# Second block's first mixer: another order of its projections, and the values' projection dealt out between attention steps

## The chip, the cores and the metric

The kernel runs on one core of one Trainium2 chip. The metric is the device time of one execution in microseconds (us), the median of the timed runs. A core has TensorE (PE: matrix products into the eight banks of PSUM), VectorE (DVE), ScalarE (ACT), GpSimd (POOL) and SyncE (SP), each with its own instruction stream, and 16 DMA engines that move data between DRAM and the on-chip SBUF. The streams meet at semaphores only.

## The reference, cut to what matters

Two blocks of a transformer follow each other; the first has two layers (l = 0, 1) and 256 tokens beside 256 context tokens, width 1024. A layer is: feed-forward, mixer, feed-forward. The change is in the mixer of layer l = 1 ("M1"):

```
qx, kx, vx, ux = split(hx @ w_in, 4)          # 512 columns each; g = 0, 1, 2, 3 below
kc, vc = split(hc @ w_in[:, 512:1536], 2)     # the context: keys and values only, in layer 1
qx, kx = axial_rope(qx), axial_rope(kx)
out = concat([attention(qx, kx, vx, kc, vc, rpb), pool_mix(ux)]) @ w_out
```

The attention has 8 heads of 64, 256 queries against 256 + 256 keys, with a bias table and a mask. `pool_mix` takes windowed means of u and multiplies each of four groups by a 128x128 matrix.

## The kernel before, in words

**Weights.** All weights come in one stream of units of 1 MB (a matrix of 512 columns is two units, the upper and the lower 512 rows). SP loads a unit into one of two `raw` buffers (`fetch`, L2807), ScalarE makes its high part (L1255) and VectorE its low part (L1883). High and low parts have three buffers (CUT = 3). A load into a `raw` buffer waits for the low part made from what was there; a cut waits until the unit three places ahead is used up. Each engine's program calls `through()` where a unit is used up, and makes there the cuts that this permits. So a cut stands in order between the engine's other work, and the place of the `through()` call sets when it comes.

**Products.** Each projection tile is 128 tokens by 512 columns: 8 parts (k steps) of three matmuls (L542 to L544: low x high, high x low, high x high). Tiles 0 and 1 are tokens, 2 and 3 context. In M1 the values and keys have four tiles, the queries and the pool input two.

**Order in M1.** `MIX_ORDER = (2, 0, 1, 3)`: values first (their tiles lie between the transposes of the boundary before, `begin`), then queries, then keys (`project`), and the pool input (g = 3) is dealt out in parts between attention steps (`u_part`). `U_AT[1] = [6, 3, 4, 3]` says how many of the 16 parts come ahead of what TensorE does in step -1, 0, 1, 2. Queries and keys of tokens are rotated: VectorE multiplies by cosines and sines (`rot`, L2200 and L2207, in the buffers XN), POOL adds the two (L2739), TensorE transposes (L832, called by `flush`), ScalarE copies to QT and KT (L1471).

**Attention.** 16 items (head, 128 queries) in 8 steps of two. In step j TensorE makes the scores of items 2j and 2j + 1 (L852), the transposes of the probabilities of items 2j - 4 and 2j - 3 (L861), and in every second step a block of products with the values (L876). VectorE adds the bias and takes the maximum (L2234 to L2242), ScalarE exponentiates (L1501), and the division is VectorE's for even heads (L2251) and ScalarE's for odd ones (L1511). The attention output is cut by ScalarE (L1543) and VectorE (L2258) over the projection's input, so it waits for the last part of the pool input. The pool's four groups stand at steps `POOL_AT[1]` = 5 and the following ones. ScalarE makes the weight cuts that a step's parts permit behind that step, VectorE behind the next one (`late`).

**POOL in M1** (its `mixer`, L2731): sums for g = 0 once rotated, then the store of a gate vector to DRAM (`gate_store`, L2709: 1024 elements of 4 bytes), then twelve loads of bias blocks (L2753, 128 KB each), the load of the pool's matrices (L2756), then the sums for g = 1. VectorE masks the bias blocks (L2215) when all have landed.

**Product behind it.** The output product of M1 follows; its four weight units are cut during the attention.

Of the kernel before, what the change touches and what calls it, by code (L numbers as in the profile page):

```python
# [167 lines left out]

MIX_ORDER = (2, 0, 1, 3)
U_AT = [[6, 2, 4, 4] + [2] * 8, [6, 3, 4, 3]]  # L170


POOL_AT = [12, 5]
EARLY = 11
# [28 lines left out]
def weight_stream(a):  # L203
# [62 lines left out]
    for l in range(2):  # L266
        push_gu(gu1[l, 0], (l, 0))
        push_down(dn1[l, 0], (l, 0))
        for g in MIX_ORDER:
# [28 lines left out]
def build(nc, a, out):  # L298
    with ExitStack() as ctx:
# [232 lines left out]
        def tensor_program(e):  # L532
# [289 lines left out]
            def mixer(l):  # L822
                n_items = 32 if l == 0 else 16
                tts = [[0, 1, 2, 3] if l == 0 or g in (1, 2) else [0, 1] for g in range(4)]
                later = []
# [10 lines left out]

                assert len(tts[MIX_ORDER[0]]) == 4
                first_unit[0] = feed.count
                begin(f"M{l}", lambda t: project_tile(f"M{l}", ("pj", l, MIX_ORDER[0]), t, t == 3))
                for g in MIX_ORDER[1:3]:  # L840
# [6 lines left out]
                def scores(n):  # L847
                    h, qt = items[n]
                    p0, hp, k0 = 64 * (h % 2), h // 2, 0 if qt < 2 else 256
                    b = bank(("sc", l, n))  # L850
                    w.wait_ge(*A.at(("tt", l, 1, tts[1][-1])))
# [55 lines left out]

                start, got, banks, last = feed.count, {}, {}, tts[3][-1]

                def u_part(p):  # L910
                    t, kt = p // 8, p % 8
                    if kt == 0:
                        banks[t] = bank(("pj", l, 3, t))
                    if kt // 4 not in got:
                        got[kt // 4] = unit(4, 512, kt // 4 - (feed.count - start))
                    n, (hi, lo) = got[kt // 4]
                    i = mm3(banks[t], (Hhi[:, kt, 128 * t:128 * t + 128], Hlo[:, kt, 128 * t:128 * t + 128]),
                            (hi[:, kt % 4, :], lo[:, kt % 4, :]), kt == 0, kt == 7)
                    if kt == 7:
                        ring.full(("pj", l, 3, t))  # L920
                        i.then_inc(*T.up(("pj", l, 3, t), *[("unit", n)] if t == last else []))
# [324 lines left out]
        def scalar_program(e):  # L1246
# [215 lines left out]
            def mixer(l):  # L1462
                n_items = 32 if l == 0 else 16
                tts = [[0, 1, 2, 3] if l == 0 or g in (1, 2) else [0, 1] for g in range(4)]
                later = []
# [9 lines left out]
                def evac(g, t):  # L1475
                    f = ("pj", l, g, t)
                    if g < 2 and t >= 2:
                        w.wait_ge(*T.at(f))
                        if g:
                            w.wait_ge(*T.at(("tt", l, 0, t))) if l == 0 else None  # L1480
# [7 lines left out]
                for g in MIX_ORDER[:3]:  # L1488
                    project(lambda t: evac(g, t), tts[g], flush, g != MIX_ORDER[0])
                    if g < 2:  # L1490
                        later.extend((g, t) for t in tts[g])
# [73 lines left out]
                def u_part(p):  # L1565
                    t, kt = p // 8, p % 8
                    if t == tts[3][-1] and kt % 4 == 3:
                        through()
# [23 lines left out]
                for i in range(-1, len(steps) + 3):  # L1592
                    done = range(p, p + (U_AT[l][i + 1] if i + 1 < len(U_AT[l]) else 0))
                    p = done.stop
                    if i < 0:
                        flush()
                    else:
                        for q in done:
                            if q % 8 == 7:
                                evac(3, q // 8)  # L1600
                        step(i)

                        for q in done:
                            u_part(q)

# [265 lines left out]
        def vector_program(e):  # L1871
# [306 lines left out]
            def project(evac, tts, ticks):  # L2178
                for u in range(2):
                    for t in tts:  # L2180
                        if ticks:
                            mod_steps(feed.tick())
                        if u:
                            evac(t)
                    through()

            def mixer(l):
                n_items = 32 if l == 0 else 16
                tts = [[0, 1, 2, 3] if l == 0 or g in (1, 2) else [0, 1] for g in range(4)]

                def evac(g, t):
# [3 lines left out]
                    w.wait_ge(*T.at(f))  # L2195
                    if g:
                        w.wait_ge(*G.at(("z", l, 0, t)))
                    w.wait_ge(*LD["rest"].at("rest"))
# [18 lines left out]

                for g in MIX_ORDER[:3]:
                    project(lambda t: evac(g, t), tts[g], g != MIX_ORDER[0])
                    if g == 1:  # L2220
                        masked(0)
# [47 lines left out]
                def u_part(p):  # L2269
                    if p // 8 == tts[3][-1] and p % 4 == 3:  # L2270
                        through()
# [414 lines left out]
        def gpsimd_program(e):  # L2686
# [44 lines left out]
            def mixer(l):  # L2731
                tts = [[0, 1, 2, 3] if l == 0 or g in (1, 2) else [0, 1] for g in range(4)]

                def evac(g):
                    for t in range(2):
                        w.wait_ge(*V.at(("rot", l, g, t)))
                        if g:
                            w.wait_ge(*T.at(("tt", l, 0, t)))
                        e.tensor_tensor(ZQ[t], XN[t][:, 0:512], XN[t][:, 512:1024], ALU.add).then_inc(  # L2739
# [4 lines left out]
                w.wait_ge(*LD["rpb"].at("rpb"))  # L2744
                evac(0)
                if l:
# [10 lines left out]
                if l == 0:  # L2757
# [217 lines left out]
```

## Time and profile before

| | us |
|---|---|
| median of 3 timed runs (2496.41 to 2496.72) | 2496.54 |
| profiled execution | 2497.18 |
| its span | 2495.4 |
| TensorE busy, share of the span | 2412.9, 97% |
| VectorE, ScalarE, GpSimd busy | 65%, 41%, 14% |
| mean granted clock of TensorE | 0.992 |

The time of an execution lies 1.8 us above its span. A timeline row gives start, duration, engine, line, operation, output<-inputs, shape and count, and in brackets the idle time before it with what released it. Matmuls are pipelined: a row of 0.39 us may be followed by the next after 0.23 us. M1 lies between 1360 and 1478 us of the span. The granted clock is a share of 2.4 GHz.

### The profile page before, as it was taken

What the parts mean: (1) busy time and instruction counts of PE and PEld (TensorE: products, weight loads), DVE (VectorE), ACT (ScalarE), POOL (GpSimd) and SP (SyncE); (2) the same over time, 40 slices, a digit from 0 to 9 for tenths busy, and PEclk for the clock granted to TensorE, in tenths of its full rate; (3) what the DMA queues carried; (4) which work ended last, traced back from release to release, by engine and by line L of the source; (5) the groups of instructions that cost most, each with busy time, mean ns of one, the idle gap of its engine ahead of it and who ended that gap; (6) DMA issues with size and microseconds to landing.
All of it is one profiled execution on the core that took longest, in us unless ns stands there. A gap on an engine that the chain in (4) does not pass through costs nothing.

```text
span 2495.4 us, 29343 instructions
## 1 busy us (share of the span) xinstructions
PE 2412.9 (97%) x12118; PEld 2004.8 (80%) x12118; DVE 1613.3 (65%) x2208; ACT 1021.2 (41%) x1431; POOL 338.9 (14%) x226
## 2 busy tenths in 40 slices
PE   7999989999999999999999989999999999999998
PEld 5887878857888778888888758887888888887987
DVE  7778686374778787543385466756566576586674
ACT  4221325365312225322225464445555544465443
POOL 0334252200143252101030200000000000000000
PEclk9999999999999999999999999999999999999999
DMA  8555552511555553544362615555544355443554
GB/s 284 185 171 184 171 173 96 156 34 57 164 174 181 164 174 120 165 138 152 103 219 92 148 52 193 186 186 163 184 128 159 118 193 190 153 142 119 187 186 142
DMA packets 242629, 385.93 MB, mean 155 GB/s; under 512 B 10880, under 2 KB 150400, under 8 KB 242432
## 3 DMA queue, kind: packets, MB, share of 16 engines
q1 hardware_dynamic: 236320, 372.43, 45.5%
q0 software_dynamic: 6176, 11.64, 2.4%
q8 instruction: 95, 1.56, 0.3%
q14 instruction: 38, 0.31, 0.0%
HBM read 382.83 MB, written 3.11 MB: 155 GB/s over the span
## 4 chain that ended last, share of the span: by engine, by line
PE 67%; DVE 17%; DMA 9%; ACT 4%; issue 3%; POOL 0%; DVEq 0%; SPq 0%; ACTq 0%
PE ps L542 17%; PE ps L544 16%; PE ps L543 16%; PE ps L548 8%; DVE arena L1906 8%; DMA raw<-in_w_mod 6%; PE ps L549 4%; DVE wlo L1883 3%; ACT whi L1255 2%; DVE arena L1903 1%; PE ps L617 1%; PE ps L876 1%; DMA grow<-gcol 1%; DMA raw<-in_w_ffn_gate_up 1%; PE ps L852 0%
## 5 line engine op out<-in xcount | busy, mean ns | idle before, releaser
L1255 ACT ACTIVATE whi<-raw 128x2048 fp32r<-128x2048 f32 x279 | 532.9, 1910 | 1122.3 <-PE ps L544 492.7
L1883 DVE TENSOR_TENSOR wlo<-raw,whi 128x2048 fp32r<-128x2048 f32 x279 | 663.3, 2378 | 489.3 <-ACT whi L1255 489.0
L542 PE MATMUL ps<-wlo,Hcut 128*128 128x512 f32 (+1 forms) x1888 | 706.2, 374 | 21.4 <-DVE Hcut L2087 13.1
L544 PE MATMUL ps<-whi,Hcut 128*128 128x512 f32 (+1 forms) x1888 | 695.9, 369 | 0.0
L543 PE MATMUL ps<-whi,Hcut 128*128 128x512 f32 (+1 forms) x1888 | 695.4, 368 | 0.0
L542 PEld LDWEIGHTS ps<-wlo,Hcut 128*128 128x128 f32 x1888 | 357.1, 189 | 89.3 <-DVE Hcut L2087 15.4
L544 PEld LDWEIGHTS ps<-whi,Hcut 128*128 128x128 f32 x1888 | 356.9, 189 | 59.8
L543 PEld LDWEIGHTS ps<-whi,Hcut 128*128 128x128 f32 x1888 | 357.4, 189 | 56.3
L542 PE MATMUL ps<-Hcut,whi 128*128 128x512 f32 (+1 forms) x1032 | 395.2, 383 | 4.9 <-DVE wlo L1883 4.9
L544 PE MATMUL ps<-Hcut,whi 128*128 128x512 f32 (+1 forms) x1032 | 394.6, 382 | 0.0
L543 PE MATMUL ps<-Hcut,wlo 128*128 128x512 f32 (+1 forms) x1032 | 394.4, 382 | 0.0
L548 PE MATMUL ps<-Hcut,whi 128*128 128x512 f32 x864 | 305.8, 399 | 0.0
L1906 DVE SCALAR_TENSOR_TENSOR arena<-raw,sc,arena 128x512 f32<-128x512 f32 x392 | 276.4, 765 | 35.1 <-DMA raw<-in_w_mod 33.1
L2696 POOL PARTITION_ALL_REDUCE arena<-arena x56 | 205.0, 3703 | 568.6 <-DVE arena L1906 376.0
L549 PE MATMUL ps<-Hcut,wlo 128*128 128x256 f32 x864 | 242.7, 281 | 0.0
L542 PEld LDWEIGHTS ps<-Hcut,whi 128*128 128x128 f32 x1032 | 193.7, 188 | 43.1 <-issue 4.2
L544 PEld LDWEIGHTS ps<-Hcut,whi 128*128 128x128 f32 x1032 | 193.5, 188 | 38.1
L543 PEld LDWEIGHTS ps<-Hcut,wlo 128*128 128x128 f32 x1032 | 193.7, 188 | 37.7
L548 PEld LDWEIGHTS ps<-Hcut,whi 128*128 128x128 f32 x864 | 162.4, 188 | 40.2
L549 PEld LDWEIGHTS ps<-Hcut,wlo 128*128 128x128 f32 x864 | 163.2, 189 | 0.0
L2110 DVE TENSOR_REDUCE arena<-ps 128x256 f32<-128x512 f32 x108 | 73.7, 687 | 23.5 <-PE ps L549 23.4
L2156 DVE TENSOR_TENSOR arena<-arena,ps 128x512 f32<-128x512 f32 x60 | 39.7, 682 | 71.9 <-PE ps L544 71.5
(269 smaller groups left out, 1806.9 us busy)
## 6 DMA issues: line engine op xcount, KB each, us to landing
raw<-in_w_ffn_gate_up SPq DMA_DIRECT2D x88, 1024.0 KB, 5.1
raw<-in_w_mod SPq DMA_DIRECT2D x65, 1024.0 KB, 5.2
raw<-in_w_ffn_down SPq DMA_DIRECT2D x44, 1024.0 KB, 4.9
raw<-in_ffn_w_in SPq DMA_DIRECT2D x44, 1024.0 KB, 5.1
raw<-in_attn_w_in SPq DMA_DIRECT2D x36, 1024.0 KB, 5.1
raw<-in_ffn_w_out SPq DMA_DIRECT2D x22, 1024.0 KB, 4.9
raw<-in_w_in SPq DMA_DIRECT2D x16, 1024.0 KB, 5.1
raw<-in_mlstm_w_in SPq DMA_DIRECT2D x12, 1024.0 KB, 5.1
```

The source lines that it names most:

```text
L542: e.matmul(o, L[0], R[1], start=start, stop=False)
L543: e.matmul(o, L[1], R[0], start=False, stop=False)
L544: return e.matmul(o, L[0], R[0], start=False, stop=stop)
L548: e.matmul(b, L[0], Hcut[:, 0, k, :], start=start, stop=False)
L549: return e.matmul(b[:, 256:512], L[1], SHORT[0][:, k, :], start=False, stop=stop)
L617: i = e.transpose(b[:, 128 * k:128 * k + 128], XS[t][:, o:o + 128], ident())
L1255: e.activation(hi_of(n), slot(n), ACT.Copy).then_inc(*A.up(("hi", n)))
L1883: e.tensor_tensor(lo_of(n), slot(n), hi_of(n).bitcast(F32), ALU.subtract).then_inc(*V.up(("lo", n)))
L1906: i = e.scalar_tensor_tensor(out=o, in0=kslot(n)[:, k, :], scalar=c, in1=o, op0=ALU.mult, op1=ALU.add)
L2110: return e.tensor_reduce(o, bk(f).rearrange("p (s n) -> p n s", s=2), AX, ALU.add)
L2156: e.tensor_tensor(AV[:, 2 * j + s, :], XN[s][:, 0:N], bk(f)[:, 0:N], ALU.mult).then_inc(*V.up(("mul", P, 2 * j + s), ("free", f)))
L2696: e.partition_all_reduce(t, t, 128, bass.bass_isa.ReduceOp.add).then_inc(*G.up(("total", l, v, h, s)))
```

## The change

In M1 the order becomes keys, queries, values, pool input. Only the first two are projected whole (`WHOLE[1] = 2`); the 32 parts of the values and the 16 of the pool input are dealt out as 8, 8, 8, 8, 4, 6, 6 parts ahead of TensorE's steps -1 to 5. The pool's groups move one step later. The buffers for the rotated sums are now written first by the keys and then by the queries, so the waits between them change places (`early_g`, `late_g`), on POOL too: the keys' sums, the gate's store, the bias blocks, the pool's matrices, the queries' sums. VectorE's rotations of the first projection now stand ahead of the first `through()`. The first block's mixer keeps its order, parts and steps.

```
-MIX_ORDER = (2, 0, 1, 3)
-U_AT = [[6, 2, 4, 4] + [2] * 8, [6, 3, 4, 3]]
-POOL_AT = [12, 5]
+MIX_ORDER = [(2, 0, 1, 3), (1, 0, 2, 3)]
+WHOLE = [3, 2]
+U_AT = [[6, 2, 4, 4] + [2] * 8, [8, 8, 8, 8, 4, 6, 6]]
+POOL_AT = [12, 6]
...
+        def part_tiles(l):
+            tts = [[0, 1, 2, 3] if l == 0 or g in (1, 2) else [0, 1] for g in range(4)]
+            return tts, [(g, t) for g in MIX_ORDER[l][WHOLE[l]:] for t in tts[g]]
...
+                order = MIX_ORDER[l]
+                early_g, late_g = [g for g in order if g < 2]
...
                 def u_part(p):
-                    t, kt = p // 8, p % 8
+                    (g, t), kt = tiles[p // 8], p % 8
+                    last, u = tts[g][-1], 2 * (g - tiles[0][0]) + kt // 4
                     if kt == 0:
-                        banks[t] = bank(("pj", l, 3, t))
-                    if kt // 4 not in got:
-                        got[kt // 4] = unit(4, 512, kt // 4 - (feed.count - start))
+                        banks[t] = bank(("pj", l, g, t))
+                    if u not in got:
+                        got[u] = unit(4, 512, u - (feed.count - start))
...
-                    else:
-                        for q in done:
-                            if q % 8 == 7:
-                                evac(3, q // 8)
+                    for q in done:
+                        if q % 8 == 7:
+                            evac(*tiles[q // 8])
+                    if i >= 0:
                         step(i)
...
-                        if u:
+                        if u if ticks else u == 0:
                             evac(t)
...
-                evac(0)
+                evac(early_g)
                 if l:
                     gate_store(1, 8)
...
-                evac(1)
+                evac(late_g)
```

## Rows read from the trace of the kernel before

**Rows 1.** Waits of TensorE, 1380 to 1500: total, times, longest

```profile
PE ps L861 <- ACT arena L1511: 7.9, 4, 3.2
```

**Rows 2.** Timeline of TensorE, 1395 to 1475

```profile
1405.28 1.03 PE L832 MATMUL ps<-cst,arena 128*128 128x128 f32 x8
...
1409.57 0.39 PE L542 MATMUL ps<-wlo,Hcut 128*128 128x512 f32 x1
...
1410.25 0.39 PE L542 MATMUL ps<-wlo,Hcut 128*128 128x512 f32 x1
...
1425.03 1.13 PE L852 MATMUL ps<-arena 64*128 64x512 f32 x4
...
1446.42 3.54 PE L876 MATMUL ps<-arena 128*64 128x256 f32 x16
...
1466.24 1.95 PE L876 MATMUL ps<-arena 128*64 128x256 f32 x16
...
1472.75 0.50 PE L542 MATMUL ps<-wlo,Hcut 128*128 128x512 f32 x1
```

**Rows 3.** Timeline of VectorE, 1370 to 1475

```profile
1377.20 2.29 DVE L1883 TENSOR_TENSOR wlo<-raw,whi 128x2048 fp32r<-128x2048 f32 x1 [1.03 <-ACT whi L1255]
...
1394.74 0.68 DVE L2200 TENSOR_TENSOR arena<-ps,cst 128x512 f32<-128x512 f32 x1
...
1396.00 0.68 DVE L2200 TENSOR_TENSOR arena<-ps,cst 128x512 f32<-128x512 f32 x1
...
1397.26 2.42 DVE L1883 TENSOR_TENSOR wlo<-raw,whi 128x2048 fp32r<-128x2048 f32 x1
...
1427.38 0.96 DVE L2215 TENSOR_TENSOR arena<-arena,cst 128x768 f32<-128x768 f32 x1 [5.83 <-DMA arena<-rpbs]
1428.44 0.42 DVE L2234 TENSOR_TENSOR arena<-ps,arena 128x256 f32<-128x256 f32 x1
...
1429.84 0.41 DVE L2234 TENSOR_TENSOR arena<-ps,arena 128x256 f32<-128x256 f32 x1
```

**Rows 4.** Timeline of ScalarE, a weight cut

```profile
1381.33 1.92 ACT L1255 ACTIVATE whi<-raw 128x2048 fp32r<-128x2048 f32 x1 [2.46 <-PE ps L544]
```

**Rows 5.** Timeline of POOL, 1114 to 1115 and 1340 to 1475

```profile
1114.25 0.90 POOL L2713 DMA_DIRECT2D grow<-gcol  x1 [14.58 <-DVE gcol L1954]
...
1396.25 4.59 POOL L2739 TENSOR_TENSOR arena<-arena 128x512 f32<-128x512 f32 x2 [29.05 <-DVE arena L2207]
1400.78 0.98 POOL L2713 DMA_DIRECT2D grow<-gcol  x1
1401.75 8.17 POOL L2753 DMA_DIRECT2D arena<-rpbs  x12
```

**Rows 6.** Line 2816, four single loads: start, then us to landing (not for 1385.6)

```profile
L2816 SPq DMA_DIRECT2D raw<-in_w_ffn_gate_up x1: 368/368/368, 1113.7 to 1113.7; - x1
...
DMA to landing us min/median/max: 5.7/5.7/5.7
...
L2816 SPq DMA_DIRECT2D raw<-in_w_mod x1: 368/368/368, 1121.8 to 1121.8; - x1
...
DMA to landing us min/median/max: 9.7/9.7/9.7
...
L2816 SPq DMA_DIRECT2D raw<-in_w_in x1: 367/367/367, 1385.6 to 1385.6; - x1
...
L2816 SPq DMA_DIRECT2D raw<-in_w_out x1: 368/368/368, 1409.8 to 1409.8; - x1
...
DMA to landing us min/median/max: 17.4/17.4/17.4
```

**Rows 7.** Two windows: busy by engine, granted clock, DMA share, GB/s

```profile
1406.00:1408.00 2.00, 2.00 (x12) 1.67 (x11) 0.52 (x1) 2.00 (x3) 2.00 (x4) 1.00 0.57 10
1447.00:1450.00 3.00, 3.00 (x16) 1.33 (x13) 2.93 (x9) 0.75 (x2) 0.00 (x0) 0.50 0.34 103
```

**Rows 8.** DMA issues of the page: count, KB each, median us to landing

```profile
raw<-in_w_in SPq DMA_DIRECT2D x16, 1024.0 KB, 5.1
```

More of the change, by code:

```diff
@@ L268, in weight_stream @@
         push_down(dn1[l, 0], (l, 0))
-        for g in MIX_ORDER:
+        for g in MIX_ORDER[l]:
             push(("cols", a["w_in"][l], 512 * g), "cut")
@@ L823, in mixer @@
                 n_items = 32 if l == 0 else 16
-                tts = [[0, 1, 2, 3] if l == 0 or g in (1, 2) else [0, 1] for g in range(4)]
+                tts, tiles = part_tiles(l)
+                order = MIX_ORDER[l]
+                early_g, late_g = [g for g in order if g < 2]
                 later = []
@@ L835, in flush @@
                     later.clear()
-                assert len(tts[MIX_ORDER[0]]) == 4
+                assert len(tts[order[0]]) == 4
                 first_unit[0] = feed.count
-                begin(f"M{l}", lambda t: project_tile(f"M{l}", ("pj", l, MIX_ORDER[0]), t, t == 3))
-                for g in MIX_ORDER[1:3]:
+                begin(f"M{l}", lambda t: project_tile(f"M{l}", ("pj", l, order[0]), t, t == 3))
+                if order[0] < 2:
+                    later.extend((order[0], t) for t in tts[order[0]])
+                for g in order[1:WHOLE[l]]:
                     project(("pj", l, g), tts[g], flush)
@@ L919, in u_part @@
                     if kt == 7:
-                        ring.full(("pj", l, 3, t))
-                        i.then_inc(*T.up(("pj", l, 3, t), *[("unit", n)] if t == last else []))
+                        ring.full(("pj", l, g, t))
+                        i.then_inc(*T.up(("pj", l, g, t), *[("unit", n)] if t == last else []))
                     elif kt == 3 and t == last:
@@ L1463, in mixer @@
                 n_items = 32 if l == 0 else 16
-                tts = [[0, 1, 2, 3] if l == 0 or g in (1, 2) else [0, 1] for g in range(4)]
+                tts, tiles = part_tiles(l)
+                order = MIX_ORDER[l]
+                early_g, late_g = [g for g in order if g < 2]
                 later = []
@@ L1487, in mixer @@
                 w.wait_ge(*V.at(("plo", f"F{l}0", NF - 1)))
-                for g in MIX_ORDER[:3]:
-                    project(lambda t: evac(g, t), tts[g], flush, g != MIX_ORDER[0])
+                for g in order[:WHOLE[l]]:
+                    project(lambda t: evac(g, t), tts[g], flush, g != order[0])
                     if g < 2:
@@ L1565, in u_part @@
                 def u_part(p):
-                    t, kt = p // 8, p % 8
-                    if t == tts[3][-1] and kt % 4 == 3:
+                    (g, t), kt = tiles[p // 8], p % 8
+                    if t == tts[g][-1] and kt % 4 == 3:
                         through()
@@ L1596, in mixer @@
                         flush()
[L1597 to L1600 removed]
+                    for q in done:
+                        if q % 8 == 7:
+                            evac(*tiles[q // 8])
+                    if i >= 0:
                         step(i)
[L1603 to L1604 removed]
+                    for q in done:
+                        u_part(q)
             def attention():
@@ L2188, in mixer @@
                 n_items = 32 if l == 0 else 16
-                tts = [[0, 1, 2, 3] if l == 0 or g in (1, 2) else [0, 1] for g in range(4)]
+                tts, tiles = part_tiles(l)
+                order = MIX_ORDER[l]
+                early_g, late_g = [g for g in order if g < 2]
                 def evac(g, t):
@@ L2216, in masked @@
                         *V.up(("bb", l, hp)))
-                for g in MIX_ORDER[:3]:
-                    project(lambda t: evac(g, t), tts[g], g != MIX_ORDER[0])
-                    if g == 1:
+                for g in order[:WHOLE[l]]:
+                    project(lambda t: evac(g, t), tts[g], g != order[0])
+                    if g == late_g:
                         masked(0)
@@ L2269, in u_part @@
                 def u_part(p):
-                    if p // 8 == tts[3][-1] and p % 4 == 3:
+                    g, t = tiles[p // 8]
+                    if t == tts[g][-1] and p % 4 == 3:
                         through()
@@ L2731, in mixer @@
             def mixer(l):
-                tts = [[0, 1, 2, 3] if l == 0 or g in (1, 2) else [0, 1] for g in range(4)]
+                tts, tiles = part_tiles(l)
+                order = MIX_ORDER[l]
+                early_g, late_g = [g for g in order if g < 2]
                 def evac(g):
```

18 lines of the change are left out of this document (9 added, 9 removed).

## The prediction, made before the result was known

> **What bounds the kernel now.** I read the page first: TensorE is busy 97% of the span, so a change can only win what TensorE still waits for, or lose by adding waits. The view of waits, cut to the second block's mixer (1380 to 1500 us), shows how much that is: the probabilities' transposes wait 7.9 us for ScalarE, in four waits of at most 3.2 us [rows 1]. TensorE's timeline places them: values, queries and keys are projected first; the first scores stand at 1425.03, the output product at 1472.75, 47.7 us later [rows 2]. In that stretch VectorE bounds: the scores of one item take it 1.40 us, from one item's first addition to the next one's [rows 3], and TensorE has only 16 projection parts to fill in, 9 of them before the first scores. VectorE began the stretch 2.4 us late, because the bias blocks landed at 1427.3 [rows 3]. After such gaps TensorE's granted clock fell to 0.50 (1.2 GHz) for 1447 to 1450 [rows 7], and sixteen values' products took 3.54 us where they take 1.95 us later [rows 2]; VectorE was the later one there, so it cost little.
>
> **The change, part by part.** No arithmetic is added or removed; the matmuls, casts and loads are the same ones in another order. All unit costs are rows: a part (three matmuls) is 0.68 us (1409.57 to 1410.25), four score matmuls, two items, 1.13 us with the overlap of the next (1.06 without), eight transposes, two items, 1.03 us, a block of values 1.95 us [rows 2]; a cut is 1.92 us on ScalarE [rows 4] and 2.29 us on VectorE [rows 3].
>
> *Front, if every load lands in time.* The first projection (four tiles) ends at 1383.5 in both kernels: it is 32 parts, 21.8 us, ahead of 1405.28, where the keys' first unit ends behind 16 parts of its own and 16 of the queries [rows 2]. After: queries 10.9 + transposes of the keys 1.7 (twice the 0.79 us that the eight of 1405.28 hold up the next matmul) put TensorE at 1396.0; 8 parts 5.5, transposes of the queries 0.8, 8 parts 5.5: first scores at 1407.8, which is 17.2 us earlier. The 48 parts now lie in the attention stretch or just ahead of it, 32 of them behind the first scores.
>
> *Attention, if every load lands in time.* TensorE's own work from the first scores on: 32 parts 21.9, scores 8.5, transposes 8.3, values 7.6, pool about 3.5 (eight small products, half a transposing pair or less each): 49.8 us. Laying the three engines' instructions out in program order, each from the end of what it waits for, with the durations above, I find these waits. (1) The pool input's second weight unit can be cut only after the values' first unit is used up, and VectorE's program does that behind its step 3: it starts the scores of items 6 and 7 at 1426.2, is through at 1429.1 and has cut at 1431.4, while TensorE is through with its step 3 at 1427.7 and stands at part 36 for 3.7 us. (2) ScalarE's first copy of attention output, at the end of its step 4 (1440.5), waits for the last part, which TensorE ends at 1443.8; VectorE stands behind it for 4.4 us, to 1444.2. (3) ScalarE then has two cuts for the output product (1448.9 to 1452.6) ahead of its step 6, VectorE waits 4.7 us for the second copy of output, to 1456.2, and makes its own two cuts to 1460.9; only then does it divide item 12. TensorE pays for (2) and (3) at the transposes of items 9, 11, 12 and 13 and at the pool's first output: 0.9 + 2.5 + 4.3 + 2.4 + 0.9 = 11.0 us. Sum: 1407.7 + 49.8 + 3.7 + 11.0 = 1472.2. The same lay-out of the kernel before ends at 1472.3 against 1472.75 in the trace. So without a late load the change is worth nothing: 17 us earlier, 17 us longer. Bounds of this term: +3 us if one more stall of the size of (1) comes up; -10 us if the waits of (2) and (3) mostly vanish, since the work alone would end at 1457.5.
>
> *Moved DMAs: the term that decides.* POOL's first rotation sum is now the keys', available as soon as the boundary ends. VectorE's last cut of the boundary starts at 1377.20 and holds it to 1379.4; two rotations, 1.26 us each (1394.74 to 1396.00), end at 1382.0 [rows 3]. POOL's sums take about 1.3 us each when nothing is in their way (the 4.59 us for two [rows 5], less the VectorE cut that held them, see below), so the second ends near 1383.5. Behind it in POOL's queue stand the gate's store (4-byte elements to DRAM) and the twelve bias-block loads, at 1400.78 and 1401.75 in the kernel before [rows 5]. They move 17.3 us up, to 1383.5. The weight load whose issue waits for the cut that ends near 1385.6 is the values' second unit. In the kernel before, the load at that place was issued at 1385.6 [rows 6] with nothing in its way, and such loads land after 5.1 us in the median [rows 8]. But the load that came 9.0 us behind the gate's store took 17.4 us, and a load 7.5 us behind another such store (1114.25 [rows 5]) took 9.7 us [rows 6]. Behind the first of these stores all DMA engines together moved 10 GB/s from 1406 to 1408 [rows 7]. Counted from the store, the two loads landed after 17.2 us and 26.4 us, the second with the bias blocks beside it. The new load is issued 2.2 us behind the store and has the bias blocks beside it. It would land between 1383.5 + 17.2 = 1400.7 and 1383.5 + 26.4 = 1409.9. I take the middle, 1405.3: its neighbours are those of the slow row, but it is issued before most of them. TensorE needs it at part 4, at 1398.7, after 4.3 us of cutting, so every microsecond beyond 1394.4 is a stall: 10.9 us (6.3 to 15.5). Queries' rotations stand behind this cut on VectorE, and their sums behind them on POOL: 0.8 us more at the transposes. Everything later shifts along, since ScalarE and VectorE stand still too. After such a gap the clock falls: the block at 1446 took 1.6 us longer than the one at 1466 [rows 2], so about 1.7 us more (0 to 3.5, none or two such stretches).
>
> The Trainium skill, page "SBUF — State Buffer", section "SBUF: two separate sides", says that VectorE with two SBUF inputs and GpSimd lock the shared port pair for a whole instruction, whoever starts first. The trace agrees: two of POOL's sums took 4.59 us at 1396 around a VectorE cut that took 2.42 instead of 2.29 [rows 3, 5]. Here POOL's second sum would start at 1382.2, the cut at 1383.3, so POOL is first and the store goes out at 1383.5; the other way round it would go out at 1386.8, behind the load.
>
> Sum: -0.1 (order) + 10.9 + 0.8 + 1.7 = +13.3 us, less 0.4 us by which my lay-out of the kernel before came out early: 12.9. The profiled execution took 2497.18 us (span 2495.4, 1.8 us around it), so the same execution would take 2510.1; the median of the timed runs is 0.64 us below the profiled one, so I forecast 2509.5 us. Its own range is 2503 to 2515 (landing 1400.7 to 1409.9).
>
> **Costed at nothing.** Copies of keys and values on ScalarE: as many as before, hidden beside TensorE's parts; uncovered each would cost less than a cut's 1.92 us [rows 4]. The bias blocks land earlier, before VectorE wants them at 1408 or with the late load; the old 2.4 us wait goes, and is inside the lay-out. The pool's one step of delay: no wait gets longer by it. First block: its order, parts and waits are unchanged.
>
> **Rivals.**
> 1. *The store does not catch the load* (POOL's second sum comes behind the cut, or 2.2 us is too short a distance). For it: a load issued at 1113.7, 0.5 us ahead of a store, landed after 5.7 us [rows 6]. Then only the pool input's first unit (issued at 1388.8) is late; it delays ScalarE's copies only if it lands after 1405. Time: 2496.5 - 0.1 with 0 to +5 on top: about 2497. Against: both stores of the rows held up what came behind them.
> The Trainium skill, page "DMA: Bandwidth & Descriptors", section "Anatomy of one DMA — SWDGE (gpsimd) path", gives a DMA about 2.0 us plus its bytes at 436 GB/s; by it 1 MB lands after 4.4 us whatever is in flight, and this rival would hold. The 17.4 us row [rows 6] is against it.
> 2. *Cover works (faster).* Place: the attention stretch. The 32 parts fill TensorE while VectorE and ScalarE run ahead, and the cuts for the output product fall into their idle time early on (VectorE has 2 to 3 us free in each of steps 1 and 2 of my lay-out). It decides if the load of the values' second unit lands within 8.8 us and waits (2) and (3) shrink from 11.0 to about 1 us: 1407.8 + 49.8 + 3.7 + 1.0 = 1462.3, 10.4 us earlier: 2486. For it: at least 7.9 us of TensorE's waits are there to win [rows 1]. Against: programs are in order, and the cuts stand where they stand.
>
> **How the numbers follow.** Late load 0.60 (2509.5), rival 1 0.20 (2497, and slower in a tenth of it), rival 2 0.18 (2486), the rest slower. What a measurement of this kernel can tell is 0.2%, 5 us: slower is above 2501.5. Slower 0.62, same 0.19, faster 0.19. The range 2492 to 2515 takes in the forecast's own range and rival 1, and leaves out most of rival 2 and the worst of late loads.
>
> **What would show it.** Right: the gate's store issued near 1383.5 and the load behind it landing after more than 9 us; one TensorE wait of 6 to 15 us in the first eight parts, released by VectorE's cut; first scores at 1414 to 1424; a further 3.7 us at the first part of the pool input's second unit; waits of 11 us in sum from the transposes of item 9 to those of item 13. Wrong: first scores at 1408 and no wait before them (rival 1 or 2, told apart by the output product's start, 1472 or 1462); a store that goes out after 1385.6; or a late load that lands before 1394.4.

## The result: slower by 0.8%

| | before | after |
|---|---|---|
| median of 4 timed runs each, us | 2496.63 (2496.41 to 2499.87) | 2516.28 (2514.35 to 2521.91) |
| profiled execution (span), us | 2497.18 (2495.4) | 2514.35 (2512.6) |
| TensorE busy, mean granted clock | 2412.9 us, 0.992 | 2419.4 us, 0.988 |

The ratio after to before is 1.0078, with a 95% interval of 1.0066 to 1.009. The forecast was 2509.5 us and the range ended at 2515: the direction, the place and the late load were right, the price of TensorE's slower clock was not, and the time lies 1.3 us outside the range.

Where the 17.2 us between the two profiled executions are can be read with a ruler laid at two instructions that both kernels have: VectorE's last cut of the boundary (1377.20 before [rows 3], 1376.49 after) and the first matmul of the output product (1472.75 before [rows 2], 1489.50 after). That stretch, called M1's length below, took 95.55 us before and 113.01 us after, 17.46 more. Ahead of it the changed kernel is 0.71 us earlier, behind it 0.45 us longer.

The view of TensorE's waits in the changed kernel, 1360 to 1510 (engine and line, released by: us in total, times, longest), answers to [rows 1]. There the waits on ScalarE were 7.9 us, and one on VectorE, which [rows 1] leaves out, was 2.1:

```profile
PE ps L861 <- DVE small L2248: 2.1, 1, 2.1
```

After, in the changed kernel:

```profile
PE ps L548 <- DVE wlo L1896: 14.2, 2, 10.1
PE ps L871 <- ACT arena L1524: 4.5, 3, 1.9
PE ps L871 <- DVE arena L2266: 4.1, 1, 4.1
PE ps L913 <- ACT arena L1569: 0.5, 1, 0.5
```

The largest, 10.1 us, is new, and it has a chain behind it. On POOL's timeline after, the gate's store (L2729) follows the first two sums and stands 18.1 us earlier than in [rows 5], the bias blocks (L2771) follow it:

```profile
1380.21 2.55 POOL L2757 TENSOR_TENSOR arena<-arena 128x512 f32<-128x512 f32 x2 [13.72 <-DVE arena L2222]
1382.71 0.98 POOL L2729 DMA_DIRECT2D grow<-gcol  x1
1383.67 8.22 POOL L2771 DMA_DIRECT2D arena<-rpbs  x12
```

The load of the values' second unit, issued 2.2 us behind the store, and the one behind it (issue, then us to landing; answers to [rows 6]):

```profile
L2834 SPq DMA_DIRECT2D raw<-in_w_in x1: 367/367/367, 1384.9 to 1384.9; - x1
...
DMA to landing us min/median/max: 19.1/19.1/19.1
...
L2834 SPq DMA_DIRECT2D raw<-in_w_in x1: 367/367/367, 1388.2 to 1388.2; - x1
...
DMA to landing us min/median/max: 23.9/23.9/23.9
```

The other loads of this kind take 5.1 us in the median. The load landed at 1404.1 (its issue had waited for the cut at 1382.29 to free its buffer); ScalarE's cut, VectorE's cut and TensorE's part 4 (timelines of ScalarE, VectorE and TensorE after) follow one another, and TensorE's two stalls for cuts are the rows with 10.06 and 4.18:

```profile
1404.10 1.91 ACT L1266 ACTIVATE whi<-raw 128x2048 fp32r<-128x2048 f32 x1 [17.77 <-DMA raw<-in_w_in]
```

```profile
1382.29 2.62 DVE L1896 TENSOR_TENSOR wlo<-raw,whi 128x2048 fp32r<-128x2048 f32 x1 [0.98 <-ACT whi L1266]
...
1406.04 2.29 DVE L1896 TENSOR_TENSOR wlo<-raw,whi 128x2048 fp32r<-128x2048 f32 x1 [17.87 <-ACT whi L1266]
```

```profile
1408.39 0.80 PE L548 MATMUL ps<-wlo,Hcut 128*128 128x512 f32 x1 [10.06 <-DVE wlo L1896]
...
1419.58 1.13 PE L862 MATMUL ps<-arena 64*128 64x512 f32 x4
...
1444.21 0.79 PE L548 MATMUL ps<-wlo,Hcut 128*128 128x512 f32 x1 [4.18 <-DVE wlo L1896]
...
1451.23 1.13 PE L862 MATMUL ps<-arena 64*128 64x512 f32 x4
...
1477.23 0.98 PE L871 MATMUL ps<-cst,arena 128*128 128x128 f32 x4 [4.13 <-DVE arena L2266]
...
1479.99 1.12 PE L871 MATMUL ps<-cst,arena 128*128 128x128 f32 x4 [1.77 <-ACT arena L1524]
1481.03 3.48 PE L886 MATMUL ps<-arena 128*64 128x256 f32 x16
```

First scores came at 1419.58 (1425.03 in [rows 2]), so 5.4 us of the 17 us head start were left; 69.9 us later, against 47.7, came the output product. The windows of the changed kernel (us; busy of PE, PEld, DVE, ACT, POOL; granted clock; DMA share; GB/s) show the two things that the reader should take away. Behind the store hardly any data moves: 15 GB/s from 1384 to 1395, although the DMA engines count as busy for 0.67 of that time, and none from 1386 to 1388. And behind the waits of 10.06, 4.18 and 4.13 us TensorE goes on at 0.50 of its clock, 1.2 GHz:

```profile
1384.00:1395.00 11.00, 11.00 (x59) 9.34 (x58) 3.20 (x2) 2.33 (x2) 8.66 (x13) 1.00 0.67 15
1386.00:1388.00 2.00, 2.00 (x10) 1.66 (x9) 2.00 (x1) 0.33 (x1) 2.00 (x4) 1.00 0.00 0
...
1403.00:1406.00 3.00, 0.00 (x0) 0.00 (x0) 0.00 (x0) 1.90 (x2) 0.00 (x0) 0.50 1.06 225
1410.00:1412.00 2.00, 2.00 (x7) 1.52 (x6) 0.86 (x3) 0.00 (x0) 2.00 (x2) 0.50 1.04 375
1445.00:1450.00 5.00, 5.00 (x14) 3.83 (x13) 1.92 (x3) 0.27 (x1) 0.00 (x0) 0.50 0.93 341
1478.00:1482.00 4.00, 2.23 (x12) 1.31 (x12) 2.69 (x8) 3.48 (x9) 0.00 (x0) 0.50 0.94 331
```

### The profile page after: what moved, and what is told of

Its sections match the earlier page's. It is cut to its first block, busy times and chain, and to the rows that moved or that the text cites. A ratio compares the mean times of both kernels' runs of the same rounds, so it can differ in the third digit from the quotient of the medians.

```text
span 2512.6 us, 29336 instructions
## 1 busy us (share of the span) xinstructions
PE 2419.4 (96%) x12118; PEld 2008.6 (80%) x12118; DVE 1613.7 (64%) x2208; ACT 1021.5 (41%) x1431; POOL 335.2 (13%) x226
## 4 chain that ended last, share of the span: by engine, by line
PE 74%; DVE 13%; DMA 6%; ACT 4%; issue 2%; DVEq 0%; SPq 0%; ACTq 0%
PE ps L548 19%; PE ps L550 19%; PE ps L549 19%; PE ps L554 8%; DVE arena L1919 6%; DMA raw<-in_w_mod 4%; PE ps L555 4%; DVE wlo L1896 3%; ACT whi L1266 2%; DVE arena L1916 1%; PE ps L623 1%; DMA raw<-in_w_in 1%; PE ps L886 1%; PE ps L862 1%; DMA raw<-in_w_ffn_gate_up 1%
```

## The experiments

M1's length is taken between the same two instructions in every kernel; medians are of the timed runs, the ratio is to the kernel before on the same chip. Three chips were used, with the kernel before at 2493.90 (experiments 1 to 3), 2493.99 (6 to 9) and 2493.43 (4, 5, 10 and 11); times of different chips are compared by their distance from it. Ahead of M1 all kernels run the same instructions, and yet VectorE's last cut of the boundary starts anywhere from 1373.4 to 1378.7 in the profiled executions, latest in experiment 1. So M1's length is the surer measure of an edit; a median can hold some us that arise ahead of M1.

| kernel | M1's length, profiled | median, us | ratio and interval |
|---|---|---|---|
| before | 95.55 | | 1 |
| after, again | 113.33 | 2511.37 | 1.0069 [1.0056, 1.0081] |
| after, store first | 101.76 | 2503.32 | 1.0031 [1.0021, 1.0042] |
| after, bias blocks late | 109.21 | 2507.35 | 1.0049 [1.0036, 1.0063] |
| before, store first | 92.65 | 2492.26 | 0.9991 [0.9982, 1.0] |
| before, store at the load | 97.98 | 2497.90 | 1.0014 [1.0005, 1.0023] |
| store first, stall of part 36 filled | 100.44 | 2499.71 | 1.003 [1.0018, 1.0041] |
| after, both stalls filled | 118.18 | 2518.35 | 1.0099 [1.0085, 1.0113] |
| store first, parts reordered | 94.28 | 2493.39 | 1.0 [0.9991, 1.0009] |
| store first, one cut late | 99.50 | 2497.07 | 1.0014 [1.0005, 1.0023] |
| store first, parts and cuts placed | 89.19 | 2486.61 | 0.9977 [0.9967, 0.9986] |
| before, store first, one cut late | 92.12 | 2490.07 | 0.9985 [0.9976, 0.9994] |
| parts and cuts placed, bias behind store | 95.32 | 2493.57 | 1.0 [0.9991, 1.0009] |

**1. The store out of the way (after).** In POOL's mixer the gate's store is put ahead of the keys' sums; it needs none of them.

```
+                if l:
+                    gate_store(1, 8)
                 evac(early_g)
-                if l:
-                    gate_store(1, 8)
```

> The changed kernel with one line moved: POOL stores the gate vector at the head of M1's mixer (about 1366 us of the span, when no weight load is in flight) instead of behind the keys' sums. Theory (the store of 4-byte elements holds up the load issued 2.2 us behind it): that load lands within 9 us instead of 19.1, TensorE's 10.1 us wait at the fourth part of the values is gone with the slow clock behind it, first scores near 1407 instead of 1419.6; the waits and slow stretches later in the attention stay, so about 2514.4 - 10.1 - 1.7 = 2502 or a little less (2498 to 2503). Rival (the bias blocks beside the load, or the new order itself, cause the wait): the load still takes over 15 us and the time stays above 2511.

Measured: 2503.32 us. The store went out at 1368.73, and the load of the values' second unit, issued at 1387.1, landed after 9.6 us instead of 19.1; TensorE's wait at part 4 was 0.46 us. The bias blocks, from 1384.85 on, were still beside it.

```profile
L2834 SPq DMA_DIRECT2D raw<-in_w_in x1: 368/368/368, 1387.1 to 1387.1; - x1
...
DMA to landing us min/median/max: 9.6/9.6/9.6
```

What follows: without the store in front of the load the stall is all but gone, and M1 is 11.3 us shorter. But 6.2 us of M1 against the kernel before remain, where the prediction had nothing: the waits behind the first scores were the same as after (4.18, 0.79, 1.91, 0.52, 4.13, 1.66).

**2. The bias blocks away from the load (after).** The queries' sums directly behind the store, the bias blocks behind them.

```
                 evac(early_g)
                 if l:
                     gate_store(1, 8)
+                    evac(late_g)
...
-                evac(late_g)
+                    evac(late_g)
```

The last line now belongs to an `if l == 0:` that stands above it; the loads of the bias blocks and the pool's matrices lie between the two places.

> The changed kernel with the store where it is, but the twelve bias blocks and the pool's matrices issued behind the queries' sums, so that the store is alone with the values' second unit. Theory (store): the load still takes long, by the row of 1121.8 it lands about 17 us after the store, 14 to 15 us after its issue instead of 19.1; TensorE waits 5 to 6 us there. The bias blocks come some 15 us later and may delay the first scores' additions. About 2508 to 2512. Rival (bias blocks): the load lands in 5 to 6 us and that wait is gone, 2500 or less.

Measured: 2507.35 us. Store at 1380.19, load issued 2.2 us behind it as in the changed kernel, with no bias block in flight (they were issued at 1405.00):

```profile
L2835 SPq DMA_DIRECT2D raw<-in_w_in x1: 367/367/367, 1382.4 to 1382.4; - x1
...
DMA to landing us min/median/max: 12.5/12.5/12.5
```

TensorE waited 3.36 us at part 4. So of the 14 us by which the load was late the store alone makes 7.4, the bias blocks with it the other 6.6. Moved back, the blocks hold up something else: they landed at 1420.1, 8.8 us behind the first scores at 1411.24, and VectorE stood still for them:

```profile
1420.09 0.96 DVE L2230 TENSOR_TENSOR arena<-arena,cst 128x768 f32<-128x768 f32 x1 [16.17 <-DMA arena<-rpbs]
```

So M1 was still 109.21 long.

**3. The same in the kernel before: the store early, and the store at a load.** The first moves `gate_store` ahead of `evac(0)`; the second does that too but lets it wait for the end of the first projection, so that it goes out where the change had put it (the wait in the diff is the second kernel's alone).

```
                 if l:
+                    w.wait_ge(*T.at(("pj", 1, 2, 3)))
                     gate_store(1, 8)
                 evac(0)
```

> The kernel before with the store at the head of M1's mixer. Theory: its bias blocks no longer stand in the stall behind the store; they land before the first scores, and VectorE starts the attention stretch 2.4 us earlier: 2494 to 2495 against 2496.6. Rival (the store is harmless, the bias blocks are slow by themselves): 2496.6, blocks land as late as before.

> The kernel before, with only the store moved to the time it has in the changed kernel (behind the values' last tile, about 1384), everything else in the old order. Theory: the load issued near 1385.6 lands 14 to 19 us later instead of 5.0, although no bias block is near it (they follow at 1401). The old order needs that unit only at 1406, so the time moves little: 2494 to 2499. Rival (bias blocks or order cause it): that load lands after 5 us.

Measured: 2492.26 and 2497.90 us. With the store at 1364.27 the output product's load, issued 9.0 us behind the first bias block, took 9.6 us instead of 17.4 [rows 6]; the bias blocks landed at 1413.2, ahead of the first scores at 1422.08, and M1 was 2.9 us shorter. In the timed runs that is 1.6 us, and the interval reaches 1. With the store at 1382.81 the load behind it, at 1384.2, took 13.4 us with no bias block about:

```profile
L2817 SPq DMA_DIRECT2D raw<-in_w_in x1: 368/368/368, 1384.2 to 1384.2; - x1
...
DMA to landing us min/median/max: 13.4/13.4/13.4
```

All DMA engines together moved 20 GB/s in the 11 us behind this store and 403 GB/s soon after:

```profile
1383.00:1394.00 11.00, 11.00 (x50) 9.13 (x49) 3.43 (x2) 2.40 (x2) 0.76 (x1) 1.00 0.22 20
1395.00:1399.00 4.00, 4.00 (x19) 3.34 (x18) 0.00 (x0) 1.38 (x1) 0.00 (x0) 1.00 1.05 403
```

What follows: the effect doesn't need the new order. A load just behind this store lands 14.7 or 14.8 us after it (13.4 + 1.4 here, 12.5 + 2.2 in the second experiment); with the bias blocks too 21.3 us (after) or, further back in the queue, 26.4 us (before). The old order loses less by it: no part waits for the unit, but VectorE's cut of it comes at 1399.57, the rotations and POOL's sums behind it come later, the transposes wait 3.3 us for them, and M1 is 2.4 us longer. The kernel before shows the same behind other stores of this kind: with two of them about 1 us apart and no bias block near, a load issued at 716.9, 3.9 us behind the second, took 13.9 us, while one issued at 439.9, 12.0 us behind, took 5.0.

**4. The changed kernel once more.**

> The changed kernel as it is, beside the kernel before on this chip. In the first comparison its four runs were 2514.35, 2515.06, 2517.5 and 2521.91. Theory (the landing of the values' second unit behind the gate's store varies from run to run): the median lies between 2512 and 2518 and the load lands 17 to 22 us after its issue. Rival (what stood above the profiled execution was one chip's doing): median within 1 us of the profiled execution, whose span is again near 2512.6.

Measured: 2511.37 us (2508.66 to 2512.68, 5 runs) against 2493.43, 17.9 us slower; span 2509.6; the load, issued 2.2 us behind the store, took 18.9 us, TensorE waited 9.83 and 4.18 us. The level of both kernels is 3 to 5 us lower on this chip, the difference is that of the profiles (17.2). The 19.65 us between the first medians hold some 2 us that the profiled execution doesn't show and this chip doesn't repeat.

**5. What the clock costs: the stalls filled.** In a stall TensorE multiplies the identity by itself into the next free bank, results unread.

```
                 def u_part(p):
+                    if l and p in (4, 36):
+                        nb, before = ring.queue[0]
+                        if before is not None:
+                            w.wait_ge(*freed(before))
+                        warm(ps[nb], 80 if p == 4 else 30)
```

> The changed kernel, and on TensorE two blocks of small matmuls whose results nobody reads: 80 in the wait ahead of part 4, 30 in the wait ahead of part 36, each into the bank that the next tile would take. They keep TensorE busy while it waits for a cut; nothing else changes. Theory (the clock term was mis-sized: parts behind the two stalls run at 0.50 of the clock and that costs about 6.5 us): the windows 1410 to 1412 and 1445 to 1450 show 1.00, the time is 4 to 7 us below the changed kernel's. Rival (most of the slow matmuls lie beside VectorE's and ScalarE's chain, which sets the end of that stretch): the clock is full there and the time 0 to 3 us lower; then the first scores come 1 to 2 us earlier and the transposes wait longer by the rest.

Measured: 2518.35 us, 7 us slower than the changed kernel in experiment 4. The timeline of TensorE says why: the blocks were far too long. Each of these matmuls stands as two in the trace, 0.113 us each, so 80 took 18.02 us for a stall of 10:

```profile
1397.36 18.02 PE L630 MATMUL ps<-cst 128*128 128x128 f32 x160
1415.14 0.48 PE L548 MATMUL ps<-wlo,Hcut 128*128 128x512 f32 x1
...
1424.42 1.13 PE L862 MATMUL ps<-arena 64*128 64x512 f32 x4
...
1444.71 6.86 PE L630 MATMUL ps<-cst 128*128 128x128 f32 x60
1451.33 0.48 PE L548 MATMUL ps<-wlo,Hcut 128*128 128x512 f32 x1
...
1455.60 1.13 PE L862 MATMUL ps<-arena 64*128 64x512 f32 x4
...
1485.41 3.46 PE L886 MATMUL ps<-arena 128*64 128x256 f32 x16
```

The cuts waited for were ready at 1407.6 and 1449.0, so the blocks overshot by 7.5 and 2.4 us. As a time the kernel tells little; as a measurement of the clock term it is the best of all, because the same work stands behind both stalls at full clock. Its windows:

```profile
1415.00:1425.00 10.00, 10.00 (x52) 7.92 (x50) 1.30 (x2) 2.05 (x4) 0.00 (x0) 1.00 0.31 107
...
1451.00:1456.00 5.00, 5.00 (x26) 3.91 (x26) 0.76 (x3) 0.60 (x1) 0.00 (x0) 1.00 0.97 397
```

From part 4 to the first scores: 9.28 us here, 11.19 in the changed kernel (1408.39 to 1419.58), so 1.9 us go to the clock. From part 36 to the next scores: 4.27 us here, 7.02 there (1444.21 to 1451.23), 2.75 us. Experiment 4, on this chip, gives 2.2 and 2.9 for the two. From those scores to the output product both take the same (38.25 and 38.27 us): nothing of what part 36 loses is given back, and nothing hid it. The rival expected, that VectorE's and ScalarE's chain sets the end there, falls.

The third place, not filled here, lies behind the wait of 4.13 us. From the last wait (1479.99) TensorE waits for nothing up to the output product. The kernel of experiment 9 runs the same instructions there at full clock; its row stands second:

```profile
1479.99:1489.50 9.51, 9.51 (x59) 6.42 (x59) 2.50 (x7) 6.24 (x15) 0.00 (x0) 0.78 0.19 60
1457.27:1464.78 7.51, 7.51 (x58) 5.46 (x59) 2.45 (x7) 5.97 (x15) 0.00 (x0) 1.00 0.01 2
```

That is 2.0 us more. The sum of the three is 6.7 us.

**6. The stall of part 36 alone filled, with the store first.** The block of 30 of experiment 5, in the kernel of experiment 1.

> On top of a1_store_first: 30 extra small matmuls (about 0.1 us each) into a free bank, ahead of part 36, where TensorE waits 4.2 us for the pool input's second weight unit. Theory (the slow clock behind that wait is a cost of its own): the granted clock stays at 1.0 over the six parts and scores behind it, which took some 2.7 us more than at full clock; the attention stretch shrinks from 69.5 to about 67 us, the time is some 2.5 us below a1_store_first, about +5.5 us against the kernel before. Rival (VectorE's chain sets that stretch, the clock is hidden): no change against a1, +8 to +9 us.

Measured: 2499.71 us, M1 1.3 us shorter than in experiment 1. Of these, 0.7 us lie ahead of the first scores (the values' load took 8.8 us instead of 9.6) and 0.6 behind them. Its block too took 6.86 us, 2.4 us beyond the cut, which ate nearly all that the clock gave back. By itself M1's length looks as if the clock mattered little; only the lengths of experiment 5 show that a gain and a loss had cancelled.

**7. The pool input's parts reordered (with the store first).** First both tiles' parts on its first unit, then both tiles' on its second, so that the second is wanted four parts later and the first is used up four parts earlier.

```
-            return tts, [(g, t) for g in MIX_ORDER[l][WHOLE[l]:] for t in tts[g]]
+            order = [(g, t, kt) for g in MIX_ORDER[l][WHOLE[l]:] for t in tts[g] for kt in range(8)]
+            if l:
+                order[-16:] = sorted(order[-16:], key=lambda x: x[2] // 4)
+            return tts, order
...
```

> On top of a1_store_first: the pool input's 16 parts in another order, the first weight unit's four parts of both tiles, then the second unit's, so that the second unit is first needed at part 40 instead of 36. Theory: the wait of 4.2 us there becomes 1.5 us and the slow clock behind it mostly goes: 4 to 5.5 us below a1, +3 to +5 us against the kernel before. Rival (the waits only move): the later waits grow by as much, +8 us.

Measured: 2493.39 us, no difference from before, where experiment 1 was 9.4 us slower. M1 is 7.5 us shorter. TensorE's waits in this kernel, 1380 to 1490:

```profile
PE ps L874 <- ACT arena L1527: 4.1, 2, 2.1
PE ps L551 <- DVE wlo L1899: 2.9, 2, 1.5
PE ps L874 <- DVE arena L2269: 1.3, 1, 1.3
PE ps L843 <- POOL arena L2760: 0.5, 1, 0.5
```

No wait is over 2.1 us, and the half-clock stretch behind part 36 is gone with its wait (4.18 to 1.45 us). Two blocks of values behind the remaining waits still ran slow (3.17 and 2.90 us for 1.95).

**8. One cut for the output product moved (with the store first).** The last of its weight cuts behind the attention loop instead of ahead of item 12's division, on ScalarE and on VectorE.

```
-                    u_part(q)
+                    if l == 0 or q < 47:
+                        u_part(q)
+            if l:
+                u_part(47)
...
```

> On top of a1_store_first: of the two cuts for the output product that ScalarE and VectorE make ahead of the last four attention items, the second is put behind the attention (ScalarE 1.9, VectorE 2.3 us). Theory: TensorE's wait for item 12 (4.1 us) shrinks by about 2 us, the wait for the copy of output ahead of it by as much on VectorE: 2 to 4 us below a1, +5 to +7 us against the kernel before. Rival (those waits come from ScalarE's order alone or from the clock): same as a1.

Measured: 2497.07 us, 3.1 us slower than before, where experiment 1 was 9.4. From the first scores to the output product TensorE takes 3.9 us less than in experiment 1 (65.5 for 69.5): the wait of 4.13 us became 1.93, and the one of 1.91 is gone. M1 is only 2.3 us shorter because the late load took 11.3 us instead of 9.6 and part 4 waited 2.11 us instead of 0.46. So this one cut made up 3.9 us of the waits that the prediction calls (2) and (3). The values' products behind the waits of 1.93 and 1.82 us took 3.51 us, as slow as behind the one of 4.13: the clock falls behind shorter waits too.

**9. Both, and the first cuts in an idle place.** Experiments 7 and 8 together, and on both engines the cuts that became possible are made in step 4, ahead of that step's division. VectorE's side:

```
+                    if l and j == 4:
+                        through()
                     if 0 <= j - 3 < len(steps):
                         values(j - 3)
...
```

> On top of a1_store_first: the reordering of c1, the last cut behind the attention as in c2, and the cut of the other unit put into the time in which ScalarE and VectorE wait for the last part of the pool input (step 4, ahead of the first copy of attention output). Theory: waits (1), (2), (3) and the slow clock behind them shrink together, 9 to 13 us below a1, so -4 to 0 us against the kernel before: from here the dealt-out values may pay. Rival (the order itself costs): still +4 us or more.

Measured: 2486.61 us, ratio 0.9977 [0.9967, 0.9986]: faster than the kernel before by 7.4 us and than the change by about 25. First scores at 1409.73, output product at 1464.78. The attention window of this kernel, and below it that of the changed one:

```profile
1409.73:1464.78 55.05, 50.91 (x281) 34.38 (x281) 38.88 (x84) 38.67 (x76) 0.00 (x0) 1.00 0.18 66
```

```profile
1419.58:1489.50 69.92, 56.61 (x282) 37.65 (x281) 41.14 (x85) 40.50 (x77) 0.00 (x0) 0.90 0.19 68
```

The same 281 or 282 matmuls keep TensorE busy 50.9 us at a clock of 1.00 and 56.6 us at 0.90: 5.7 us of the 14.9 between them are matmuls running slower, the other 9.2 are waits. Of the 5.7, experiment 5 counts 2.75 and 2.0; the rest lies ahead of the last wait, where it need not cost time. The busy VectorE differs by one cut, moved out of the window.

**10. Is it the order, or the cuts?** Before, with the store first and its last cut for the output product (behind part 15) moved behind the loop in the same way.

> The kernel before with two edits: the gate's store ahead of the first rotation sums on POOL, and the last cut for the output product (behind part 15) made behind the attention loop on ScalarE and VectorE. Theory (cuts in the attention stretch cost both orders the same: 1.92 us of ScalarE and 2.29 us of VectorE in a chain that bounds): 2 to 4 us less than with the store alone (2492.3), about 2489 to 2490, the three waits on ScalarE near 3 us instead of 5. Rival (the old order's chain is bound by VectorE's scores alone and the cut fell into a gap): within 1 us of 2492.3. If it comes out at 2486.6 or less, the new order with placed cuts owes nothing to the order.

Measured: 2490.07 us, 0.9985 [0.9976, 0.9994], 3.4 us faster than before; M1 0.5 us shorter than with the store alone, and the two intervals overlap. The first two waits on ScalarE were 2.71 and 2.15 us instead of 2.71 and 0.55, the one on VectorE fell from 1.53 to 0.16. So the old order has little to win by this cut: it had been beside other waits. Against the kernel before, experiment 9 stands 4.0 us lower than this one, and its M1 is 2.9 us shorter. How much of that is the order's stays open: the old order was not given its pool input's parts by unit nor the other cut's new place, and the two intervals overlap.

**11. The bias blocks behind the early store (in experiment 9's kernel).** `gate_store`, then the twelve loads, then the keys' sums.

> The changed kernel with the store first, the pool input's parts by unit and the cuts placed (2486.6), and besides the twelve bias blocks issued directly behind the store, ahead of the keys' sums on POOL. Theory (what still makes the load of the values' second unit late, 11.4 us, is the bias blocks' packets beside it): the bias blocks have landed by 1390, the load takes 5 to 7 us, the wait of 2.3 us at part 4 goes, and the time is 2 to 3 us lower, 2484. Rival (the store itself holds everything behind it for some 17 us, whatever stands there): the bias blocks land as late as before and the load still takes over 9 us; time within 1 us of 2486.6, or above if weight loads of the boundary, issued from 1372 on, are now the late ones.

Measured: 2493.57 us, 7 us slower than experiment 9 and no difference from before. The bias blocks landed at 1389.0, as the theory had it, but the load of the values' second unit still took 10.9 us, and the time is the one that the rival had for late loads of the boundary: the load issued 3.4 us behind the last bias block is now late too, and the last four of the keys' transposes wait 5.92 us for a copy that stands behind the cut of it on ScalarE:

```profile
L2852 SPq DMA_DIRECT2D raw<-in_w_in x1: 368/368/368, 1376.6 to 1376.6; - x1
...
DMA to landing us min/median/max: 14.4/14.4/14.4
```

```profile
1393.48 1.12 PE L843 MATMUL ps<-cst,arena 128*128 128x128 f32 x4 [5.92 <-ACT arena L1497]
```

Store at 1364.10, landing at 1391.0: 26.9 us, the 26.4 us of the kernel before again. Together the store and the blocks held up the load behind them here as well. In experiment 9 they stand 16 us apart, the load behind the blocks took 11.4 us, and no wait of TensorE was over 2.3 us.

## Why the prediction was right in kind and short in size

*Moved DMAs.* Right. Store at 1382.71 (forecast 1383.5), load issued at 1384.9 (1385.6), landed at 1404.1 (1405.3), TensorE's stall 10.06 us (10.9). That the landing came so close is in part luck: 1405.3 was the middle between two rows 9.2 us apart. POOL's second sum did come ahead of VectorE's cut, which took 2.62 us instead of 2.29. The 0.8 us more at the transposes did not come. Rival 1 is ruled out, and with it the 4.4 us per load: the Trainium skill, page "DMA: Bandwidth & Descriptors", section "Anatomy of one DMA — SWDGE (gpsimd) path", gives its sum for DMAs that GpSimd issues. This load is SyncE's, takes 5.1 us in the median and took 19.1 here, and the measurement decides. Experiments 1 to 3 show the cause by taking the store away, the blocks away, and by making the same late load in the old order.

*Waits (1), (2) and (3).* Right in place; 4.18 us for 3.7 at part 36, and 9.1 us for 11.0 behind it; together 13.3 for 14.7.

*The clock.* This is the step that failed, in size: "about 1.7 us more (0 to 3.5, none or two such stretches)". There were three such stretches, behind the waits of 10.06, 4.18 and 4.13 us, and they cost 1.9, 2.75 and 2.0 us, 6.7 us in all (experiment 5; the last by the same instructions in experiment 9). The prediction named these three waits itself, at 10.9, 3.7 and 4.3 us, and it had the price in a row [rows 7]; it let only one stretch lose, by the price of one block of values in the kernel before, where VectorE was later anyhow. The kernel before even had a second slow block, which the prediction did not read:

```profile
1456.83 3.62 PE L876 MATMUL ps<-arena 128*64 128x256 f32 x16
```

Behind the first two waits of the changed kernel parts run, not a block: at half clock each takes 1.28 us (three matmuls, 0.43 apart) instead of 0.68, and TensorE was the later engine.

*The order by itself.* "Without a late load the change is worth nothing" was wrong by the same step. With the load's stall down to 0.46 us M1 is 6.2 us longer than before and the kernel slower, 1.0031 [1.0021, 1.0042] (experiment 1). About 4.3 us of it are the two clock stretches that remain (2.5 and 1.8 us in this kernel), 1 us the waits of 0.46 and 0.51 us at part 4 and at the queries' transposes.

The sum, for the profiled executions: forecast +12.9, found +17.2. Of the 4.3 between them the clock is +5.0 (6.7 for 1.7), the stall -0.8, the order and all else in M1 +0.4 (17.46 - 10.06 - 6.7 = 0.7 for 0.3), the rest of the program -0.3. With 5.0 us more in the clock term the forecast would have been 2514.5. Most of the +0.4 is a slip of the sum: it took off 0.4 us because the lay-out of the kernel before ended early, but a lay-out that ends early for both kernels leaves their difference as it is. The last 2 us to the median lie between executions and stay open.

*Rival 2*, that cover works, describes what the order can do, but not as changed: it needed an earlier load, the parts of the pool input by unit, and two cuts in other places on both engines. Experiment 9 is 7.4 us faster than before, the rival had 10.4; that both come out near 2486 is chance, since the kernel before ran 2.6 us lower on that chip.

## What to carry to other kernels

When work is moved in a program in order, list the DMAs that stand behind it in the same queue, and what is loaded within 15 to 27 us of each store like the gate's: here taking a 4 KB store out of the way gave back 11.3 of the 17.5 us that M1 had grown by. Price TensorE's long waits twice, once as the wait and once as the work behind it at half clock: 1.9 to 2.75 us more each here, where TensorE was the later engine. Shorter waits close together did it too (3.18 and 2.42 us in the kernel before, 1.93 and 1.82 in experiment 8). And if work is dealt out as cover, deal out by when its buffers become free, and place the cuts for the product behind it where their engines idle; that made a loss of 18 us a gain of 7.

## What the hardware showed unexpectedly

- A store of 1024 elements of 4 bytes held up 1 MB loads on another queue although its issue takes 0.98 us: the load landed 14.7 and 14.8 us behind the store, 21.3 us with twelve bias blocks of 128 KB beside it, and 26.4 and 26.9 us where it came later; alone such a load takes 5.1 us. Behind the store all DMA engines together moved 15, 20 and 27 GB/s for 11 us (the changed kernel, the store at the load, the bias blocks late), and 0 from 1386 to 1388 in the changed kernel. No run changed the size of the store's elements, so it is not shown that their size is what counts.
- The bias blocks without the store near: 8.8 to 11.4 us for the load issued 2.2 us behind the first of them (five kernels with the store first), 9.6 for one issued 9 us behind (experiments 3 and 10).
- At half clock the same six parts and their transition to the scores took 7.02 us instead of 4.27, and nothing of it came back in the 38 us that followed, although TensorE waited 9 us in them. That fits waits which each count from what TensorE itself delivers to VectorE and ScalarE; no run tested that reason.
